# Key norms inverted once per token and head, decays read one token back, and a new order of the products between the mixer's projection and its chunks

## The reference

```python
w = -jax.nn.softplus(-(w0 + jnp.tanh(xw) @ w_up)) - 0.5
decay = jnp.exp(-jnp.exp(w.astype(jnp.float32)))
a = jax.nn.sigmoid(a0 + xa @ a_up)
g = jax.nn.sigmoid(xg) @ g_up
kk = (k * k_k).astype(jnp.float32).reshape(B, S, H, N)
kk = kk / jnp.maximum(jnp.linalg.norm(kk, axis=-1, keepdims=True), 1e-12)
k = k * (1.0 + (a - 1.0) * k_a)
...
y = _rwkv7_scan(rh, hs(decay), kh, vh, -kk, kk * ah)
...
bonus = jnp.sum(rh * kh * r_k.astype(jnp.float32), axis=-1, keepdims=True)
y = y + bonus * vh
return (y.reshape(B, S, RWKV_WIDTH) * g.astype(jnp.float32)).astype(f.dtype)
```

## Time and profile before

| what | value |
|---|---|
| median of 3 runs | 2297.89 us |
| the profiled execution's own time | 2296.89 us |
| its span | 2295.1 us |
| PE busy, share of the span | 95% |
| DVE | 70% |
| ACT | 55% |
| POOL | 14% |
| mean granted TensorE clock | 0.979 |
| PE's share of the chain that ended last | 79% |

### The profile page before, as it was taken

The page is one execution under the profiler, slowest core; times in us unless marked ns, Lnnn a source line. Parts: engine busy times, 40 slices in busy tenths (PEclk is TensorE's granted clock), DMA queues, the critical chain, the costliest instruction groups (busy, mean ns, idle before and its releaser), DMA issues.

```text
span 2295.1 us, 55123 instructions
## 1 busy us (share of the span) xinstructions
PE 2184.8 (95%) x21760; PEld 1948.0 (85%) x21760; DVE 1604.7 (70%) x3080; ACT 1102.1 (48%) x1891; POOL 329.4 (14%) x164
## 2 busy tenths in 40 slices
PE   8897999999999999999898889999999999999997
PEld 8786999988888888788696869999888888887885
DVE  6645697786666667975566448978766666679754
ACT  5533455444444444445464334554444444445443
POOL 0020698000000000000000216970000000000000
PEclk9899999999999999999998989999999999999998
DMA  6212345434444444445341123544344444444451
GB/s 250 92 40 75 129 166 184 145 129 164 164 166 167 168 171 157 159 159 190 127 149 73 40 92 129 178 170 147 129 164 164 164 166 166 169 158 154 166 193 63
DMA packets 46617, 335.03 MB, mean 146 GB/s; under 512 B 5168, under 2 KB 5296, under 8 KB 6320
## 3 DMA queue, kind: packets, MB, share of 16 engines
q1 hardware_dynamic: 46512, 333.61, 40.5%
HBM read 332.54 MB, written 1.05 MB: 145 GB/s over the span
## 4 chain that ended last, share of the span: by engine, by line
PE 79%; DVE 7%; POOL 6%; issue 6%; ACT 1%; DMA 0%; POOLq 0%; SPq 0%; DVEq 0%; ACTq 0%
PE PS L1626 31%; PE PS L1603 23%; PE PS L1311 8%; PE PS L1615 6%; POOL low L432 5%; PE PS L1327 4%; PE PS L1518 1%; PE PS L1475 1%; DVE low L1084 1%; PE PS L1509 1%; PE PS L1299 1%; DVE rnorm L943 1%; DVE hot L1154 1%; DVE hot L1150 1%; PE PS L1343 0%
## 5 line engine op out<-in xcount | busy, mean ns | idle before, releaser
L651 ACT CAST high<-ring 128x1024 fp32r<-128x1024 f32 x512 | 535.6, 1048 | 602.7 <-PE PS L1603 444.4
L1603 PE MATMUL PS<-hTh,high 128*128 128x256 f32 x2048 | 594.7, 290 | 12.7 <-ACT GA L655 10.9
L1603 PE MATMUL PS<-hTh,low 128*128 128x256 f32 x2048 | 578.8, 283 | 0.0
L1603 PE MATMUL PS<-hTl,high 128*128 128x256 f32 x2048 | 577.2, 282 | 0.0
L1084 DVE TENSOR_TENSOR low<-ring,high 128x1024 fp32r<-128x1024 f32 x432 | 515.5, 1220 | 0.8 <-ACT high L651 0.6
L1603 PEld LDWEIGHTS PS<-hTh,high 128*128 128x128 f32 x2048 | 387.2, 189 | 17.4 <-ACT GA L655 9.7
L1603 PEld LDWEIGHTS PS<-hTl,high 128*128 128x128 f32 x2048 | 387.5, 189 | 0.0
L1603 PEld LDWEIGHTS PS<-hTh,low 128*128 128x128 f32 x2048 | 387.5, 189 | 0.0
L1626 PE MATMUL PS<-high,WH 128*128 128x512 f32 x1024 | 323.8, 397 | 0.0
L1626 PE MATMUL PS<-low,WH 128*128 128x512 f32 x1024 | 318.0, 392 | 0.0
L1626 PE MATMUL PS<-high,WL 128*128 128x512 f32 x1024 | 316.4, 390 | 0.0
(11 more groups left out here) (245 smaller groups left out, 3020.5 us busy)
## 6 DMA issues: line engine op xcount, KB each, us to landing
ring<-in_peer_slabs SPq DMA_DIRECT2D x256, 1024.0 KB, 4.8
ring<-in_w_slabs SPq DMA_DIRECT2D x58, 1024.0 KB, 4.8
xres<-in_x SPq DMA_DIRECT2D x2, 512.0 KB, 4.6
out<-obuf SPq DMA_DIRECT2D x2, 512.0 KB, 2.6
cst<-in_consts SPq DMA_DIRECT2D x1, 680.0 KB, 10.5
praw<-in_p_t SPq DMA_DIRECT2D x1, 512.0 KB, 15.1
gfin<-in_g_final SPq DMA_DIRECT2D x1, 512.0 KB, 5.6
vec<-in_vecs SPq DMA_DIRECT2D x1, 356.0 KB, 7.3
```

Of the source, the lines that this page charges most:

```text
L651: act.copy(high[:, (c0[L] + j) % DEEP], ring[:, place, half * D:(half + 1) * D]).then_inc(part_hi, 1)
L1603: ins = mm(PS[:, 6 + j % 2, 0:SEQ], u[:, b, ks], h[:, k], start=n == 0, stop=n == 3 * KT - 1)
```

## The change

- **Key norms.** VectorE forms `kk` first and squares it (`sqk`); ScalarE's squares and root, VectorE's 128x1024 clamp and reciprocal go. TensorE sums the squares the other way round, `sqk` as stationary operand and two columns of `ones2` as moving one, so that tokens lie on partitions and the sums are 16 columns (8 heads, 2 blocks of tokens). VectorE clamps 128x16, GpSimd raises it to the power -1/2 (`knrm`), and TensorE spreads it back to channels by 16 products with the identity, each writing 64 partitions, into banks 6 and 7. VectorE multiplies `kk` with these banks.
- **Decays.** `cprev` and `wprev` go. The exponential is written into `wedge`, which has 65 columns for each chunk, the first of them 1; `ar` reads columns 0 to 63 for "one token back" and 1 to 64 for "this token".
- **Order.** The `a` and decay products are made right behind the attention transposes, before the sums of squares; the gate product comes after the spreading. ScalarE's tanh stands ahead of `hTh`, two table loads are pulled ahead by one-column activations, the gate's sigmoid stands behind the others and `gT` behind the exponentials. Banks move accordingly. Both `keep_warm` calls of the stage go.
- **Bonus.** `rkprod` is formed behind the operands of the chunk products; its sum on TensorE stands behind the chunk products and ahead of the inverse, `bonus_v` behind the fourth identity add, and the second half of level 0's transposes waits for it, since they share banks 6 and 7.
- **Masks.** GpSimd makes level 0 of `Mt` for all four groups, then level 1. `Mt` and `X` lie in separate tiles.

```diff
+TOK_BANKS = (2, 6, 4)
+PROD_BANKS = (0, 1, 2, 3, 6, 7, 4, 5)
...
-        cprev = place("cprev", M + 2048, [4, SEQ])
-        wprev = place("wprev", M + 4096, [4, SEQ])
+        wedge = place("wedge", M + 2048, [4, NCHUNK, CHUNK + 1])
...
+                pool.wait_ge(kss_max, L + 1)
+                pool.tensor_tensor(knrm, knrm, minus_half.broadcast_to([P, TB * NH]), ALU.pow).then_inc(knorm, 1)
...
                 for g in range(4):
                     pool.wait_ge(prod_ready, 8 * L + 2 * g + 2)
-                    for lv in range(2):
-                        pool.tensor_tensor(Mt[:, lv, 4 * g:4 * g + 4], prods[:, 4 * g:4 * g + 4, 0], level(lv, 4), ALU.mult).then_inc(mt_ready, 1)
+                    pool.tensor_tensor(Mt[0][:, 4 * g:4 * g + 4], prods[:, 4 * g:4 * g + 4, 0], level(0, 4), ALU.mult).then_inc(mt_ready, 1)
+                for g in range(4):
+                    pool.tensor_tensor(Mt[1][:, 4 * g:4 * g + 4], prods[:, 4 * g:4 * g + 4, 0], level(1, 4), ALU.mult).then_inc(mt_ready, 1)
...
+                act.activation(xw_t[0:64], fm[0:64, T_LORA], ACT.Tanh).then_inc(lora_in, 1)
                 for k in range(4):
                     act.wait_ge(aoT_ps, 2 * L + k // 2 + 1)
...
-                    ins = act.activation(sqk[:, t], fm[:, 4 + t], ACT.Square, scale=V[:, C_KK + t:C_KK + t + 1])
...
-                act.activation(rnorm[:], rnorm[:], ACT.Sqrt).then_inc(knorm, 1)
...
+                act.activation(stat[:, 151:152], minus_half, ACT.Sigmoid)
...
+                act.activation(xg_s[:, :, :], fm[:, T_GATE:T_GATE + 2], ACT.Sigmoid).then_inc(lora_in, 1)
+                act.activation(stat[:, 150:151], minus_half, ACT.Exp)
...
+                act.activation(wedge[:, :, :, 1:], csum[:].rearrange("p t (c s) -> p t c s", c=NCHUNK), ACT.Exp, scale=-EXP_MINUS_HALF).then_inc(decay_ready, 1)
...
-                act.activation(wprev[:], cprev[:], ACT.Exp, scale=-EXP_MINUS_HALF).then_inc(decay_ready, 1)
...
+                act.wait_ge(lora_ps, 3 * L + 3)
+                act.copy(gT[:], PS[:, 2:4].rearrange("p a (b c) -> p (a b) c", b=2)).then_inc(g_ready, 1)
...
+                dve.tensor_tensor(sqk[:], kk[:], kk[:], ALU.mult).then_inc(sqk_ready, 1)
+                dve.memset(wedge[:, :, :, 0:1], 1.0)
...
-                dve.tensor_scalar(rnorm[:], PS[:, 6:8].rearrange("p a (b c) -> p (a b) c", b=2), 1e-24, None, ALU.max).then_inc(kss_max, 1)
-                dve.wait_ge(knorm, L + 1)
-                dve.reciprocal(rnorm[:], rnorm[:]).then_inc(kk_ready, 1)
+                dve.tensor_scalar(knrm, PS[:, 6, 0:TB * NH], 1e-24, None, ALU.max).then_inc(kss_max, 1)
...
-                dve.tensor_tensor(cprev[:], csum[:], sw[:], ALU.subtract).then_inc(csum_ready, 1)
...
+                dve.wait_ge(rn_ps, L + 1)
+                link(dve.tensor_tensor(kk[:], kk[:], PS[:, 6:8].rearrange("p a (b c) -> p (a b) c", b=2), ALU.mult))
...
+                dve.scalar_tensor_tensor(arv[:, :, 0], halves(kk), -1.0, edges[:, :, :, 0:CHUNK], ALU.mult, ALU.mult)
...
-                keep_warm(6, 4)
...
+                pe.wait_ge(sqk_ready, L + 1)
+                for tb in range(TB):
+                    for t in range(4):
+                        o = tb * NH + 2 * t
+                        ins = mm(PS[:, 6, o:o + 2], sqk[:, t, tb * P:(tb + 1) * P], ones2[:, 0:P:HD], start=True, stop=True)
+                ins.then_inc(kss_ps, 1)
+                pe.wait_ge(knorm, L + 1)
+                for t in range(4):
+                    for tb in range(TB):
+                        o, at = tb * NH + 2 * t, (t % 2) * SEQ + tb * P
+                        for e in range(2):
+                            ins = mm(PS[half(e), 6 + t // 2, at:at + P], knrm[:, o + e:o + e + 1].broadcast_to([P, HD]), ident, start=True, stop=True)
+                ins.then_inc(rn_ps, 1)
...
-                        keep_warm(2, 4)
...
                 pe.wait_ge(prod_ready, 8 * (L + 1))
+                pe.wait_ge(rk_ready, L + 1)
+                for n in range(2):
+                    ins = mm(PS[:, 6 + n], ones2, rkprod[:, 2 * n:2 * n + 2].rearrange("p a b -> p (a b)"), start=True, stop=True)
+                ins.then_inc(bonus_ps, 1)
...
+                        if lv == 0 and g:
+                            pe.wait_ge(bonus_ready, L + 1)
```

More of the change, by code:

```diff
@@ L196, in hybrid_encoder @@
         PT1 = place("PT1", R + 14336, [NH, 2, P])
-        wcum = place("wcum", R + 10240, [4, SEQ])
         ar = place("ar", R + 11264, [4, TB, 2, P])
@@ L417, in _ @@
                         pool.wait_ge(m_ps, 4 * (LEVELS - 1) * L + 4 * (lv - 2))
-                    pool.tensor_tensor(Mt[:, lv % 2], prods[:, :, 0], level(lv, 16), ALU.mult).then_inc(mt_ready, 1)
+                    pool.tensor_tensor(Mt[lv % 2][:], prods[:, :, 0], level(lv, 16), ALU.mult).then_inc(mt_ready, 1)
                 norm(3 * L + 1)
@@ L590, in _ @@
                         act.wait_ge(x_ps, 4 * ((LEVELS - 1) * L + lv) + g + 1)
-                        act.copy(X[:, 4 * g:4 * g + 4], four(PS[:, 4 + g, 0:4 * CHUNK])).then_inc(x_made, 1)
+                        act.copy(X[L][:, 4 * g:4 * g + 4], four(PS[:, 4 + g, 0:4 * CHUNK])).then_inc(x_made, 1)
                     if lv:
@@ L954, in _ @@
                 link(ins)
-                link(dve.scalar_tensor_tensor(kmod[:], kmod[:], 1.0, fm[:, 4:8], ALU.add, ALU.mult))
+                dve.scalar_tensor_tensor(kmod[:], kmod[:], 1.0, fm[:, 4:8], ALU.add, ALU.mult)
+                dve.wait_ge(rn_ps, L + 1)
+                link(dve.tensor_tensor(kk[:], kk[:], PS[:, 6:8].rearrange("p a (b c) -> p (a b) c", b=2), ALU.mult))
+                link(dve.tensor_tensor(bvec[:], kk[:], avec[:], ALU.mult))
+                dve.wait_ge(decay_ready, 2 * (L + 1))
+                halves = lambda t: t[:].rearrange("p a (b c s) -> p (a b) c s", b=TB, c=2)
+                edges = wedge[:].rearrange("p t (b c) s -> p (t b) c s", b=TB)
+                dve.tensor_tensor(bt[:], bvec[:], winv[:], ALU.mult)
+                dve.tensor_tensor(kt[:], kmod[:], winv[:], ALU.mult).then_inc(bkt_ready, 1)
+                arv = ar[:].rearrange("p a b q (c s) -> p (a b) q c s", c=2)
+                dve.scalar_tensor_tensor(arv[:, :, 0], halves(kk), -1.0, edges[:, :, :, 0:CHUNK], ALU.mult, ALU.mult)
+                dve.tensor_tensor(arv[:, :, 1], fm[:, 0:4].rearrange("p a (b c s) -> p (a b) c s", b=TB, c=2), edges[:, :, :, 1:], ALU.mult).then_inc(bkt_ready, 1)
                 for t in range(4):
@@ L1427, in _ @@
                 ins.then_inc(lora_ps, 1)
-                pe.wait_ge(kss_max, L + 1)
-                pe.wait_ge(rk_ready, L + 1)
-                for n in range(2):
-                    ins = mm(PS[:, 6 + n], ones2, rkprod[:, 2 * n:2 * n + 2].rearrange("p a b -> p (a b)"), start=True, stop=True)
-                ins.then_inc(bonus_ps, 1)
                 pe.wait_ge(gates_ready, 2 * (L + 1))
```

92 lines of the change are left out of this document (33 added, 59 removed).

## The result

| | before | changed |
|---|---|---|
| median, same chip (4 runs each) | 2298.46 us (2294.98 to 2299.71) | 2277.46 us (2274.93 to 2279.51) |
| ratio of the medians | | 0.9911 [0.9893, 0.9928] |
| the profiled execution's own time | 2296.89 | 2274.93 |
| its span | 2295.1 | 2273.1 |
| mean granted clock | 0.979 | 0.985 |

The change saves 21.0 us by these medians. The forecast was 2279, so time and sign were right. The steps behind it were only partly right, and the experiments say which.

The account below looks back on a forecast made before the run. The prediction took the stage as bound by a chain over four engines, priced by the clock. 11.5 us gained less 1.9 for the bonus made 9.6 a layer, 19.2 in two: 2279 us, range 2268 to 2294.

Parts of the forecast that it names:

- T: Point where all eight banks of prods are done: 130.7 in layer 0 before, forecast 119.2, 11.5 us earlier.
- The path through the reciprocal: Key norms: VectorE's reciprocal, 6.55 us on the path, goes; sums of squares done at 95.6, csum scans start about then.
- The power: GpSimd's power on 128x16 clamped sums: 2.5 us by the slope of two small sizes, bounds 0.7 and 9.1.
- The spreading: TensorE's 16 products (32 passes) after the power: halves overlap, 1.7 us at full clock; taken at half clock, 3.4.
- VectorE behind it: After the spreading: six full-size operations of 1.2 us from kk to ar, ending at 109.2; scans and kmod hidden.
- The gate: Eight gate products on TensorE behind the spreading: 5.0 us at full clock, ending at 107.0; 9.2 at half.
- Rival B: Clock stays at half through the gate: 9.2 us there, 4.5 us gained a layer, 2289; chance 0.29 with the dear power.
- The refill "costs nothing": SyncE gets the low-rank slab back at about 107; no cost, since the slab it loads is used 70 us later.
- The bonus: Moves onto the path behind T: 8.4 us to the inverse's level-1 product, 6.55 before; 1.9 us lost a layer.
- Masks and strided reads: GpSimd's new order has level 0 done 2 us sooner; strided reads of wedge cost nothing.
- Elsewhere: Rest of the layer: same work, moved; low-clock stretches may change by a few us either way.
- Rival D: Power costs 0.7 us, clock holds, VectorE's 108 is late: 13.3 us gained a layer, 2270; chance 0.08.

Follow-up runs that it names:

- norms alone: The kernel before with only the new key norms (16-column sums, clamp, GpSimd's power, spreading); zeros, cprev and old bonus stay: median 2285.61 us, ratio 0.9959.

## Why the prediction was right, step by step

The forecast was a gain of 19.2 us, 9.6 a layer, and nothing elsewhere. Measured in the spans were 16.1 in the stages and 5.9 elsewhere. So the total was right within 3 us by the spans for two errors of opposite sign, which is luck, and the trace must be held against each term. Layer 1's 9.6 is not the forecast's 9.6 either: T came 9.6 us earlier there, not 11.5, and the bonus cost nothing, not 1.9.

- **The path through the reciprocal** was right. It was the bound, the scans started at 94.94 (forecast 95.6), the sums of squares were done at 94.8 (95.6), and norms alone gave 4.0 and 4.6 us.
- **The power** was mis-sized: 3.35 us, not 2.5. One, two and 16 columns took 0.57, 0.70 and 3.35, that is 0.19 for each further column, where the slope of the two small sizes gave 0.13. The value lay inside the bounds of 0.7 and 9.1. Cost: 0.85 a layer.
- **The spreading** was right with both of its choices: half clock behind the gap, and overlapping halves. 3.68 was measured for 3.4, 1.97 for 1.7 without the gap. The Trainium skill (TensorEngine Tiling (Array Packing), Key Properties) says the tiles work independently, and the trace agrees: 0.062 us a pass at full clock, where eight full-width loads of 128 columns took 0.86, 0.107 each.
- **VectorE behind it** was right: the second half of `ar` ended at 109.4, for 109.2. VectorE was idle for 2.57 us before `kk`, as the timeline of the changed kernel has it, so `kmod` and the scans did hide behind the power:

```profile
102.23 1.22 DVE L948 TENSOR_TENSOR kk<-kk,PS 128x1024 f32<-128x1024 f32 x1 [2.57 <-PE PS L1419]
```

- **The gate** was near: 5.6 us, for 5.0. The first step still ran at half clock (1.15), then the clock came back behind the spreading, as forecast. In layer 1 all but the first, at 0.69, were 0.63 apart. Rival B, half clock through the gate, did not happen. The token transposes were priced at full clock, 4.0 us; in layer 1 they took 5.13, at a granted clock of 0.67.
- **The refill "costs nothing"** was the step that failed. The prediction asked when the slab is used, 70 us later, not what its transfer delays. The transfer itself did not move, but the token transposes came beside it. So its 1 MB stood in front of a 16 KB fetch of TensorE's instructions, and TensorE stopped for 3.00 us in layer 0: the first masks came at 117.02 and T at 122.6, for 113.3 and 119.2.
- **The bonus** was priced too dear: 1.9 us a layer. From T to the product with `XT` it is 7.56 in layer 0 (forecast 8.4, before 6.55) and 6.56 in layer 1, as before. The wrong piece was the clock. The products were put at half clock, 3.57 us; in layer 0 they took 2.50, partly at half clock, in layer 1 2.00, at full clock. And the 6.55 us before, read as "half of it at half clock", had a granted clock of 0.58, so 5.5 us of them were at half. At an equal, full clock the bonus costs 1.5 us there.
- **Masks and strided reads.** The strided reads were rightly priced at nothing. The masks' new order did not have the last of level 0 done 2 us sooner: the fourth identity add ends 1.9 us behind T in both kernels. It gave 0.3 us a layer ahead of T instead.
- **Elsewhere** was priced at zero, with "a few us either way" in the last paragraph. It is 5.9 us: 0.65 at the head, less 0.9 between the stages, and 6.2 behind them, 2.2 of it from two stops that the kernel before has and the changed one has not, and most of the rest from 9.7 us less half clock. That term was missing. Nothing in the prediction says which way it would go; it was luck that it made good the 3.1 that the stages gave less than forecast.

Rival D (power at 0.7, 2270) comes close to the run without the root, which has 0.27 us in the power's place: 2271.45. Its mechanism was right in layer 0, where the clock held and the spreading took 1.97; in layer 1 the spreading took 3.26.

## What to carry to other kernels

Cut the span at points that every version has and judge an edit by its own stage: here a local gain of 3 us that the stage's trace shows plainly (the later refill) did not appear in the total at all, since the half-clock time elsewhere changed. Compare a piece with and without an edit at the same granted clock: the bonus's place looks free at 6.56 against 6.30 us and costs 1.5 at an equal clock. When a transfer and a stage of many small products come to stand side by side, by whichever is moved, ask what the transfer's bytes will stand in front of, instruction fetches among them, and not only when they are needed. Filler work on the chain is worth less than it occupies there: 7.1 us of zeros in each layer gave 1.5 and 1.9 when taken out, since the squares were late next and the sums lost the clock.

## What the runs showed of the hardware that I had not expected

- A fetch of 16 KB of instructions, TensorE's by what stops, comes only behind a bulk transfer of 1 MB that is under way: it landed at 112.43 to 113.39 behind a transfer from 108.79 to 112.43, and TensorE stood for 3.00 us. With the transfer later it came at 109.74 and cost nothing. TensorE went on 1.2 to 1.4 us after the landing in all six such traces, so the stop is shorter when TensorE comes to it late. The kernel before has two more of these stops (0.95 and 0.68 us) in its layer 1.
- GpSimd's power is not flat in the columns: 0.57 us for 128x1, 0.70 for 128x2, 3.35 for 128x16.
- The clock's price outside the stage is somewhat under 0.5 us for each us at half clock (0.47 and 0.44 by the two fits). Seen over the whole span, the traces of these two kernels had 70 to 104 us of it, and the same kernel twice 97 and 104, or 70 and 80.
